# DeltaNet layer: six filler matmuls of a head moved from the first transpositions into the recurrence

## The reference

```python
def step(S, inp):
    qc, kc, vc, gc, bc = inp
    G = jnp.cumsum(gc, axis=-1)
    decay = jnp.exp(jnp.where(tri, G[..., :, None] - G[..., None, :], -jnp.inf))
    lmat = jnp.where(strict, bc[..., :, None] * jnp.einsum('bhik,bhjk->bhij', kc, kc) * decay, 0.0)
    eg = jnp.exp(G)
    rhs = bc[..., None] * (vc - eg[..., None] * jnp.einsum('bhck,bhkv->bhcv', kc, S))
    u = lax.linalg.triangular_solve(eye + lmat, rhs, left_side=True, lower=True, unit_diagonal=True)
    o = eg[..., None] * jnp.einsum('bhck,bhkv->bhcv', qc, S) + jnp.einsum(
        'bhij,bhjv->bhiv', jnp.einsum('bhik,bhjk->bhij', qc, kc) * decay, u)
    tail = jnp.exp(G[..., -1:] - G)
    S_new = jnp.exp(G[..., -1])[..., None, None] * S + jnp.einsum('bhck,bhcv->bhkv', kc * tail[..., None], u)
    return S_new, o
```

## Time and profile before

| | |
|---|---|
| runs of before, median (lowest to highest) | 4041.88 us (4040.19 to 4042.70) |
| the profiled execution: its own time, its span | 4042.75 us, 4041.1 us |
| instructions | 54777 |
| TensorE matmul / weight load busy | 94% / 73% of the span |
| VectorE, ScalarE, GpSimd busy | 45%, 23%, 30% |
| mean granted TensorE clock | 0.975 of full |

### The profile page before, as it was taken

One profiled execution on the slowest core, in us unless ns is written; L12 is line 12 of the kernel. 1 busy time (PEld: TensorE's weight loads), 2 busy tenths in 40 slices (PEclk: granted clock), 3 DMA queues, 4 the chain that ended last, 5 costly groups with the idle time before them and its releaser, 6 DMA issues. The chain is left out here.

```text
span 4041.1 us, 54777 instructions
## 1 busy us (share of the span) xinstructions
PE 3807.0 (94%) x20290; PEld 2931.7 (73%) x20290; DVE 1802.4 (45%) x2980; ACT 943.6 (23%) x2138; POOL 1207.4 (30%) x1021
## 2 busy tenths in 40 slices
PE   8999999998899999999999888989979999999999
PEld 5666666666677888878867766666657688887887
DVE  4565556655443111136661226666655411112666
ACT  3333332333210000000001015555631100000001
POOL 0111011111142333323331106656633233332432
PEclk9999999998699999999999999999989999999999
DMA  4111011111231111123332220000033111112322
GB/s 149 33 38 38 27 34 36 38 38 27 72 98 54 42 42 42 42 88 103 92 121 59 68 74 2 1 2 1 1 95 94 66 42 42 42 42 64 109 86 80
DMA packets 322017, 223.99 MB, mean 55 GB/s; under 512 B 28442, under 2 KB 313235, under 8 KB 319827
## 3 DMA queue, kind: packets, MB, share of 16 engines
q1 hardware_dynamic: 316164, 214.99, 18.0%
q0 software_dynamic: 2048, 5.25, 0.5%
q10 hardware_dynamic: 3650, 1.64, 0.2%
HBM read 191.54 MB, written 34.37 MB: 56 GB/s over the span
## 5 line engine op out<-in xcount | busy, mean ns | idle before, releaser
L775 PE MATMUL ps<-xT,work 128*128 128x272 f32 x2688 | 643.4, 392 | 0.0
L775 PEld LDWEIGHTS ps<-xT,work 128*128 128x128 f32 x2688 | 510.7, 190 | 105.3
L1320 PE MATMUL ps<-xn,work 128*128 128x363 f32 (+1 forms) x1536 | 547.2, 475 | 6.8 <-issue 6.7
L775 PE MATMUL ps<-xn,work 128*128 128x272 f32 x2016 | 489.9, 392 | 3.9 <-DVE work L846 3.9
L775 PEld LDWEIGHTS ps<-xn,work 128*128 128x128 f32 x2016 | 382.9, 190 | 83.9 <-issue 5.1
L387 PE MATMUL ps<-work 128*128 128x272 f32 x1676 | 404.3, 398 | 13.4 <-PEq L1155 7.3
L387 PEld LDWEIGHTS ps<-work 128*128 128x128 f32 x1676 | 321.8, 193 | 84.3 <-issue 17.2
L2946 POOL TENSOR_SCALAR work<-work 128x640 f32<-128x640 f32 (+4 forms) x192 | 313.6, 1643 | 196.7 <-DVE work L2849 196.4
L1320 PEld LDWEIGHTS ps<-xn,work 128*128 128x128 f32 x1536 | 260.7, 191 | 105.5 <-issue 21.4
L648 POOL TENSOR_TENSOR xT<-xT,work 128x272 f32<-128x272 f32 x96 | 198.3, 2078 | 253.2 <-DVE work L512 164.4
L2032 POOL TENSOR_TENSOR xT<-xT,consts 128x512 f32<-128x512 f32 x96 | 127.6, 1336 | 451.9 <-DVEq L1859 391.3
(11 more groups left out here) (425 smaller groups left out, 5841.4 us busy)
## 6 DMA issues: line engine op xcount, KB each, us to landing
work<-in_ffn_w_in_dram SPq DMA_DIRECT2D x88, 512.0 KB, 5.1
xn<-in_ffn_w_out_dram SPq DMA_DIRECT2D x46, 704.0 KB, 4.5
work<-in_gdn_w_in_dram SPq DMA_DIRECT2D x32, 512.0 KB, 4.2
work<-in_ffn_w_out_dram SPq DMA_DIRECT2D x18, 704.0 KB, 4.5
ffn_parked_residual<-xT SPq DMA_DIRECT2D x2, 4352.0 KB, 13.7
work<-in_gdn_w_out_dram SPq DMA_DIRECT2D x32, 256.0 KB, 2.8
work<-in_nsa_w_out_dram SPq DMA_DIRECT2D x64, 128.0 KB, 2.9
xT<-ffn_parked_residual SPq DMA_DIRECT2D x4, 1632.0 KB, 10.2
```

Of the source, the lines that this page charges most:

```text
L775: ins = pe.matmul(acc(a, n), w[:, k, :], t[:, k, a * SUB:(a + 1) * SUB], start=(first and k == 0), stop=(k == HK - 1), skip_group_check=True)
L1320: mm = pe.matmul(unit_acc(u, m), w[j % 2][:, k, :], c.xn[:, k, o:o + cnt], start=(k == 0), stop=(k == KD - 1))
```

## The change

The table that says how many fillers precede each step gets other numbers. The steps p1 of both groups have one filler each instead of four. dS of chunks 2, 6 and 7 have three instead of two, u of chunk 4 has two instead of one, and dS of chunk 4 has four instead of two. The sum in front of o2's end stays 101. As step_of reads the same table, the work on ScalarE, VectorE and GpSimd that is tied to counts of fillers is put at other steps of their programs too; the four taps of q, which are tied to steps, stay.

```diff
-FILL = {"p1": 4, "p2": 4, "P": 1, "Y": 1, "sP": 1, "sY": 1, "s1": 1, "s2": 1, "kS": 2, "u": 1, "dS": 2,
-        "kss": 2, "kst2": 2, "u2": 2, "o2": 4, "oss": 0, ("P", 0, 0): 5, ("sP", 0): 4}
+FILL = {"p1": 1, "p2": 4, "P": 1, "Y": 1, "sP": 1, "sY": 1, "s1": 1, "s2": 1, "kS": 2, "u": 1, "dS": 2,
+        "kss": 2, "kst2": 2, "u2": 2, "o2": 4, "oss": 0, ("P", 0, 0): 5, ("sP", 0): 4,
+        ("dS", 2): 3, ("u", 4): 2, ("dS", 4): 4, ("dS", 6): 3, ("dS", 7): 3}
```

## The result

| | before | after |
|---|---|---|
| runs, median (lowest to highest) | 4042.29 us (4040.19 to 4044.42) | 4082.08 us (4078.25 to 4082.27) |
| ratio, 95% interval | | 1.0095 [1.0079, 1.0111] |
| profiled execution: its own time, its span | 4042.75, 4041.1 us | 4081.95, 4080.3 us |
| mean granted TensorE clock | 0.975 | 0.972 |

The kernel became slower by 39.8 us. 4061 was predicted, at most 4076: the sign was right, the size about half of the true one. Before has four executions here, one more than the three ahead of the prediction.

A forecast was written before the change was run, and what follows sets the result against it. TensorE was taken as the bound, except in each head's front, set by a ScalarE and VectorE chain. 4042.75 +20.6 (fillers and stalls) -3 +2 (clock) gave 4062, less 0.9: 4061 us; range 4046 to 4076.

The forecast's parts named there:

- The front: Heads 1 to 6, ahead of L1373: taking six fillers out gains nothing; the stall grows from 0.72 to 4.4 us.
- The recurrence: First to last dS: added fillers cover little, since stalls move with the counts to kS1, u1, dS3, u4, kS5 and dS6.
- Rival 1: Fillers cover old stalls, no new ones form in the recurrence: 4030 us, chance 0.05 in full; half covered 4051, 0.12.
- Levels 1 and 2: Level 2 gets a new stall of 1.44 us behind GpSimd's wait for unit 2; level 1's 0.29 goes.
- Levels 4 and 5: Doubling levels: taps of K leave both levels, level 5's stall goes, and no new stall is listed at level 4.
- Level 5's stall (1.12) goes: Ahead of the last doubling level's L1385: the 1.12 us stall vanishes as taps of K move into the recurrence.
- The clock: Half clock: -3 us taken for falls at the heads' ends, +2 (10 at most) for falls behind the new front stall.
- Rival 2: Front idle time throws TensorE to half clock in all six heads, 1.6 us each, ends keep theirs: 4072 us, chance 0.13.
- The bound there: Heads' ends: with another head length, half-clock falls in none of them (-12.8 us) or in all (+5).
- Rival 3: Clock falls vanish at the heads' ends because of the new head length: 4051 us, chance 0.08.
- Head 0: No head before it, so TensorE gains up to 3.66 us in its front; the head as a whole unchanged.

The follow-up runs named there:

- e1: Kernel before, with six fillers a head moved from p1 to p2, still in the front, later counts as before: 4044.57 us, 1.0003 of before.
- g1: Kernel before, with three fillers a head moved from the recurrence into the front, due counts as before: 4020.19 us, 0.9936 of before.
- g2: Kernel before, fillers unmoved, with taps, silus, squares and roots tied to steps with room on their engine: 3991.18 us, 0.9870 of before.
- e4: Kernel before, TensorE's fillers unmoved, the other engines' work placed by due counts of the changed table: 4040.27 us, 0.9995 of before.
- h1: Changed kernel, with GpSimd's last-level masks held until after VectorE's last tap of q, and its edges of q's tile due later: 4055.61 us, 1.0032 of before.
- e3: Changed kernel with 16 useless matmuls in group 0's new idle time, heads 0 to 6 (output wrong, times only): 4072.98 us, 1.0075 of before.
- e2: Changed kernel, with GpSimd's first last-level mask held until VectorE has written the update that follows the last tap of q: 4050.62 us, 1.0029 of before.
- h2: The changed kernel measured once more, no edit: 4076.61 us, 1.0084 of before.

## Why the prediction was too low

**The front (right, but for a detail).** L1373 stayed 11.8 us behind the Ln, and the six fillers became idle time there. e1 and g1 show the same from both sides: in heads 1 to 6 fillers in that stretch are nearly free, taken out or put in. Of the 4.2 us of idle time forecast ahead of L1373, 3.55 stand there; 0.94 stand ahead of the second transpositions, whose wait the prediction took to be over long before.

**The recurrence (right).** Predicted per head: +3.66 of fillers, -4.8 of old stalls, +4.59 of new ones, 3.45. Measured: 45.37-41.93 = 3.44. Stall by stall, predicted and read: kS1 0.54 and 0.64, u1 0.72 and 0.81, dS3 0.78 and 0.78, u4 0.62 and 0.55, kS5 0.50 and 0.24, dS6 1.43 and 1.32; dS2, dS4 and dS7 gone. These sum to 4.34; the stretch is 0.24 longer than they and the fillers explain. Rival 1, that the fillers cover stalls and no new ones form in the recurrence, fell by these readings; g2 got rid of the old ones by moving the work that causes them. But my reading of how the counts act was too simple, as e4 shows: moved alone, they made two stalls in the recurrence, of 1.18+0.16 and 2.24+0.16 us, and not the six. Where both move, as here, the sum came out right; for the counts alone it did not.

**Levels 1 and 2 (right).** +1.15 predicted (1.44 and -0.29), +0.99 measured, the 1.44 of level 2 to the hundredth. h1 took it away by itself.

**Levels 4 and 5 (the step that failed).** "Level 5's stall (1.12) goes" counted -1.12 a head; the stretches from level 2 to u0 measured +0.84 (0.06+0.86-0.08). The stall did go from level 5, and a larger one formed at level 4. I had asked of each engine's queue what is placed ahead of what, and had not asked what runs beside what. GpSimd's masks came out from behind their wait for unit 5 and ran beside VectorE's tap of q. Both operations kept their places in their programs; their durations changed. The difference is 1.96 a head, 13.7 us in seven, two thirds of the miss. The trace of the kernel before had the sign of it: the first tap of K takes 1.78 us beside the masks (411.93), where the first tap of V beside nothing takes 0.75. The Trainium skill, GPSIMD Engine Reference, section "1. Specifications", says that GpSimd shares its SBUF interfaces with VectorE and contends with VectorE instructions that have two SBUF inputs (or run in a two-port mode). The later taps have two such inputs, and the trace agrees: 1.28 us alone, 2.31 beside the masks. The prediction's list of stalls also leaves out one that didn't move: the first products of level 4 stand for 1.09+0.16 us on VectorE (L1876) before, 1.04+0.16 after; g2 took it away.

**The clock.** Behind the idle time I took +2 and measured +4.5 (e3 gives it back whole). Rival 2 was right that all six heads would show the fall, and wrong in its price, 1.6 a head: five lost 0.57, head 1, where it lasted twice as long, 1.64, since the stall of the second group's products at the chain's end took the rest. At the heads' ends I took -3 and got -1.6. The bound there was mis-summed: with the rows' 2.9 us a fall, falls at all seven ends would be +7.5 against before, and not +5. Rival 3, no falls at all there, did not come with the change, but it came with e2: 9.60 at all ends. Ends all at full clock or not are worth some 14 us between kernels otherwise near alike, which is more than any single stall here.

**Head 0.** TensorE gained 2.33 us of 3.66. In h2 and e2, with the same table, the same front took 3.08 and 3.07 less than before. The first profile has a half-clock stretch at 32.7 us, the other two one at 21, the kernel before none; that this is the 0.7 between them is argued, not shown, and 0.6 stays open. Head 0 as a whole was forecast unchanged and became 5.9 us longer: -2.3 in its front, +5.6 from there to dS7, as in the other heads, and +2.6 at its end, where before it met no half clock.

**The sum.** Against the 39.2 us of span, 19.6 were predicted (20.6, -3 and +2). The rest: 13.7 at levels 4 and 5, -1.1 at levels 1 and 2, 0.2 in the recurrence, 2.5 and 1.4 of the clock, 1.3 in head 0, -1.4 in head 7 (+0.35+0.31+0.37-2.56+0.16), 2.8 behind the heads. That is 19.4 (0.2 is rounding). The upper end of the range, 4076, held the stalls 0.1 off each and the clock at its worst, and no new stall at a place where I had found none; a range for a change that moves work on four engines needs one.

## What to carry to other kernels

When work on one engine is the clock by which other engines' work is placed, list for both orders what each engine runs at the same moment, and not only what stands ahead of what: a wait that keeps two engines apart can be worth more than the stall it causes. A stall is removed by moving its cause to where its engine has room (g2: 1.3%), and filler work belongs where a chain of other engines sets the pace (g1: 0.6%, a third of it the clock in its profile; 1.84 us a head from g2 to g3); putting filler in front of a stall while moving the cause along with it bought nothing. Where the granted clock falls at fixed places of a loop, a saving in that loop can be taken back (h1), or doubled (e2), by where the new length puts the falls: compare the stretch that was edited before comparing totals.

## What was not expected of the hardware

- A tap on VectorE (three operands, 128x1024 floats) takes 1.28 us, and 2.31 beside GpSimd's two-operand masks; its small companion (128x64) 0.28 and 1.28. GpSimd's mask took 1.98 instead of 1.27.
- Half clock locks to the loop: in the changed kernel the falls came every head at the same two places (363.8 and 380.9, 493.5 and 510.6, 623.2 and 640.3, 752.9 and 770.0, 882.6 and 899.7), in e2 at one, and in e2 one run of ten was 24 us longer at a lower mean clock. What decides at a given head length I can't say from these runs.
- In the front TensorE stood for 3.7 us at a granted clock of 1.00, and the fall to 0.50 (510.6 to 514.0) came after it had begun again at 509.86, while it worked without a gap. In head 7 of the kernel before, with 5.49 us of idle time, it fell at 990.2, before TensorE began again at 992.07.
